# An encoder trunk: loads in another order, modulation chunks two slots later, bias masking in four pieces

## The reference

```
mod = silu(c) @ w_ada + b_ada                    # 1024 -> 6 x 1024, per sequence
sh1, sc1, gt1, sh2, sc2, gt2 = split(mod, 6)
hn = rmsnorm(x, g_mix) * (1 + sc1) + sh1
x  = x + gt1 * token_mixers(hn)
hn = rmsnorm(x, g_ffn) * (1 + sc2) + sh2
x  = x + gt2 * expert_choice_ffn(hn)
```

## Time and profile before

| | |
|---|---|
| time before, median of 3 runs | 2814.52 us (2800.98 to 2831.42) |
| profiled execution | 2833.76 us, span 2832.0 us, granted TensorE clock 0.899 |
| busy, share of the span | TensorE 87%, VectorE 66%, ScalarE 46%, POOL 13% |
| the chain that ended last, by engine | TensorE 76%, VectorE 9%, DMA 7%, issue 4% |
| DMA over the span | 599.38 MB, mean 212 GB/s |

### The profile page before, as it was taken

How to read it: one execution, slowest core, us unless ns; L and a number is a source line. 1 busy time by engine, 2 the same in 40 slices (tenths; PEclk the granted TensorE clock), 3 DMA queues, 4 the chain that set the end, 5 groups by cost and what they waited for, 6 DMA issues and landing times.

```text
span 2832.0 us, 31133 instructions
## 1 busy us (share of the span) xinstructions
PE 2469.0 (87%) x11606; PEld 1856.4 (66%) x11606; DVE 1856.3 (66%) x2984; ACT 1297.0 (46%) x2075; POOL 377.8 (13%) x253
## 2 busy tenths in 40 slices
PE   3978997969949999999969799698997699999993
PEld 1645775537737888888746467565775588888882
DVE  2535545535559999999844464454644899999994
ACT  1214323124307777777621243132431577777771
POOL 1011000101002111121100120001200011211112
PEclk8989888978969999999979797898987799999997
DMA  9055004060059999999860630322002899999994
GB/s 321 17 191 189 31 38 138 15 214 23 23 198 307 388 392 382 387 387 379 314 182 1 239 127 31 110 50 82 16 31 90 328 378 387 390 391 382 388 373 159
DMA packets 215461, 599.38 MB, mean 212 GB/s; under 512 B 36414, under 2 KB 51022, under 8 KB 215280
## 3 DMA queue, kind: packets, MB, share of 16 engines
q1 hardware_dynamic: 194496, 522.21, 49.6%
q0 software_dynamic: 15824, 58.27, 7.4%
q10 hardware_dynamic: 4992, 16.92, 1.6%
HBM read 555.62 MB, written 43.84 MB: 212 GB/s over the span
## 4 chain that ended last, share of the span: by engine, by line
PE 76%; DVE 9%; DMA 7%; issue 4%; ACT 1%; SPq 1%; POOL 1%; PEld 0%; POOLq 0%; DVEq 0%; PEldq 0%; ACTq 0%
PE bank L1407 12%; PE bank L1409 12%; PE bank L1408 12%; PE bank L1248 7%; PE bank L1317 5%; PE bank L1298 4%; DMA ring_a<-in_w_ada 3%; PE bank L1307 3%; PE bank L1341 3%; PE bank L1343 2%; PE bank L1342 2%; PE bank L1244 2%; PE bank L1246 2%; PE bank L1245 2%; DMA ring_w<-in_w_ada 2%
## 5 line engine op out<-in xcount | busy, mean ns | idle before, releaser
L1079 DVE TENSOR_TENSOR feed_lo<-feed,feed_hi 128x1024 fp32r<-128x1024 f32 x768 | 888.3, 1220 | 86.1 <-ACT feed_hi L718 84.4
L718 ACT ACTIVATE feed_hi<-feed 128x1024 fp32r<-128x1024 f32 x768 | 749.6, 1051 | 208.9 <-PE bank L1409 90.8
L1317 PE MATMUL bank<-V,pbuf 128*128 128x64 f32 x1664 | 251.5, 297 | 26.8 <-ACT pbuf L683 16.7
L1317 PEld LDWEIGHTS bank<-V,pbuf 128*128 128x128 f32 x1664 | 240.7, 219 | 39.0 <-ACT pbuf L683 25.3
L675 ACT ACTIVATE pbuf<-pbuf,smin 128x256 f32<-128x256 f32 (+2 forms) x192 | 117.3, 611 | 321.7 <-DVE smin L912 321.6
L1248 PE MATMUL bank<-ring,hT 128*128 128x512 f32 x512 | 228.3, 601 | 0.0
L476 POOL TENSOR_TENSOR stat<-stat,neg_half 128x1 f32<-128x1 f32 (+2 forms) x88 | 70.5, 801 | 1096.1 <-DVE stat L995 578.0
L1407 PE MATMUL bank<-feed_hi,hid_hi 128*128 128x512 f32 x512 | 204.9, 400 | 9.1 <-DVE hid_lo L1101 9.1
L1407 PE MATMUL bank<-feed_hi,merged_hi 128*128 128x512 f32 x512 | 207.2, 405 | 1.1 <-DVE merged_lo L1086 1.1
L1407 PE MATMUL bank<-feed_hi,xe_hi 128*128 128x512 f32 x512 | 204.9, 400 | 0.0
L1409 PE MATMUL bank<-feed_hi,merged_lo 128*128 128x512 f32 x512 | 204.1, 399 | 0.0
(11 more groups left out here) (190 smaller groups left out, 4117.4 us busy)
## 6 DMA issues: line engine op xcount, KB each, us to landing
feed<-in_w_gate SPq DMA_DIRECT2D x64, 2048.0 KB, 11.9
feed<-in_w_up SPq DMA_DIRECT2D x64, 2048.0 KB, 11.4
feed<-in_w_down SPq DMA_DIRECT2D x64, 2048.0 KB, 10.9
ring_a<-in_w_ada SPq DMA_DIRECT2D x40, 1024.0 KB, 5.2
...
X<-residual ACTq DMA_DIRECT2D x24, 512.0 KB, 3.5
...
```

What stands on the lines that cost most here:

```text
L718: act.activation(feed_hi[q % HIGHS][:, kk, :], feed[q % FEED][:, kk, :], ACT.Copy).then_inc(feed_hi_ready, 1)
L1079: dve.tensor_tensor(feed_lo[q % FEED][:, kk, :], feed[q % FEED][:, kk, :], full(feed_hi[q % HIGHS][:, kk, :]), ALU.subtract).then_inc(feed ...
L1317: ins = pe.matmul(bank[5 + oc // 512][:, oc % 512:oc % 512 + HD], pbuf[:, 3 + m % 2, b * P:(b + 1) * P], V[:, lo + b, vc:vc + HD], start=( ...
```

## The change

- First stage: the identity of `con` is loaded alone, the rest after POOL's memsets, with a semaphore of its own. X is loaded only after piece 1 has landed. The small rows are turned after the products with the pieces. `skew` is in two parts: `skew_pad` stays at the start, the writes of the DRAM table come after the first meeting.
- Masking: four instructions over 128 x 896 at slots 1, 3, 5 and 7, each of which waits until VectorE has done so many slots; VectorE waits for each at slots 12 to 15.
- Modulation chunks at slots 2n + 4 and 2n + 5, `mod_turn` at 20.
- SP after the projection: passes 1 to 3 all load the first chunk, w_out, the other chunks, then gate and rows; pass 4 as before.
- Layer seam: the chunks of w_in are loaded and, for tile 0, used in the order 1, 2, 3, 0.

In the diff, changes that only hand `it` on to `chunks` and `projected` are left out.

```diff
--- before.py
+++ after.py
@@ -102,6 +102,9 @@
 SLOTS = 16 * (TILES - 1) + AFTER[-1][0] + 1
 
 
+BIAS_AT = (1, 3, 5, 7)
+
+
 def streamed(layer, s):
 
     if s == 0:
@@ -119,15 +122,17 @@
     return 1 + layer * (SEQS + 2) + stage
 
 
-def chunks(i):
-
-
-    return (0, 1, 2, 3) if i == 0 else (2, 1, 0, 3)
-
-
-def projected(i, ch):
-
-    return MIX_CHUNKS * i + chunks(i).index(ch) + 1
+def chunks(it, i):
+
+
+    if i == 0:
+        return (1, 2, 3, 0) if it == SEQS else (0, 1, 2, 3)
+    return (2, 1, 0, 3)
+
+
+def projected(it, i, ch):
+
+    return MIX_CHUNKS * i + chunks(it, i).index(ch) + 1
 
 
 def schedule(layer, s):
@@ -136,9 +141,11 @@
     for k in range(SLOTS):
         out.append(("slot", k // 16, k))
         for n, c in enumerate(streamed(layer, s)):
-            out += [(name, c, k) for at, name in ((2 * n + 2, "ada_sum"), (2 * n + 3, "ada_turn")) if at == k]
-        if s == 0 and k == 19:
+            out += [(name, c, k) for at, name in ((2 * n + 4, "ada_sum"), (2 * n + 5, "ada_turn")) if at == k]
+        if s == 0 and k == 20:
             out.append(("mod_turn", 0, k))
+        if k in BIAS_AT:
+            out.append(("bias", BIAS_AT.index(k), k))
         for i in range(TILES):
             out += [(name, i, k) for at, name in AFTER if 16 * i + at == k]
     return out
@@ -254,7 +261,7 @@
         c_turned = sem("c_turned")
         pad_ready = sem("pad_ready")
         started = sem("started")
-        consts_in, passed = sem("consts_in"), sem("passed")
+        consts_in, rest_in, passed = sem("consts_in"), sem("rest_in"), sem("passed")
         arrived, released = sem("arrived"), sem("released")
         layer_in = sem("layer_in")
         skew_in, skew_out, bias_in = sem("skew_in"), sem("skew_out"), sem("bias_in")
@@ -374,7 +381,7 @@
 
                 for n, c in enumerate(streamed(layer, s)):
                     t = ada_turns(layer, s) + n
-                    if s == 0 and n == 1:
+                    if n == 1:
                         load_out(layer)
                     for h in range(2):
                         if n:
@@ -396,7 +403,7 @@
             for layer in range(LAYERS):
                 for s in range(SEQS):
                     it = layer * SEQS + s
-                    for n in range(MIX_CHUNKS):
+                    for n in (1, 2, 3, 0) if s == 0 and layer else range(MIX_CHUNKS):
                         if it == 0 and n >= 2:
                             sp.wait_ge(first_used, n + 1)
                         elif s == 0 and layer:
@@ -418,16 +425,13 @@
                                           [[127, GRID], [GRID * 128, 14], [1, GRID]])
                             sp.dma_start(bias_c[r * GRID:(r + 1) * GRID, h, :, :], src).then_inc(bias_in, 16)
                     sp.wait_ge(proj_used, it + 1)
-                    if s == 0:
-                        load_ada(layer, s)
-                    else:
+                    load_ada(layer, s)
+                    if not streamed(layer, s):
                         load_out(layer)
                     sp.wait_ge(mod_out, layer * 16 + 16)
                     sp.dma_start(gate[:, :], row_of(0, s, P)).then_inc(row_gate, 16)
                     sp.dma_start(rows2[:, 0, :], row_of(16, s, P)).then_inc(row_norm, 16)
                     sp.dma_start(rows2[:, 1, :], row_of(8, s, P)).then_inc(row_norm, 16)
-                    if s:
-                        load_ada(layer, s)
                 sp.wait_ge(row_used, layer * SEQS + SEQS)
                 for g in range(SEQS):
                     sp.dma_start(gate[64 * g:64 * g + 64, :], row_of(24, g, 64)).then_inc(row_gate, 16)
@@ -462,13 +466,14 @@
                 pool.sem_inc(released, 1)
 
             pool.dma_start(nat[0:2, 0:D], c[:, :]).then_inc(consts_in, 16)
-            pool.dma_start(con[:, :], consts[:, :]).then_inc(consts_in, 16)
+            pool.dma_start(con[:, 0:P], consts[:, 0:P]).then_inc(consts_in, 16)
             pool.memset(neg_half[:, :], -0.5).then_inc(started, 1)
             pool.wait_ge(started, 1)
             pool.memset(aff[:, :, :, :], 0.0).then_inc(started, 1)
             pool.wait_ge(started, 2)
             pool.memset(silu_c[:, :], 0.0).then_inc(started, 1)
             pool.wait_ge(started, 3)
+            pool.dma_start(con[:, P:C_END], consts[:, P:C_END]).then_inc(rest_in, 16)
 
             def powers(at, count, n):
 
@@ -476,15 +481,17 @@
                 pool.tensor_tensor(stat[:, 8 + at:8 + at + count], stat[:, at:at + count], neg_half[:, 0:count], ALU.pow)\
                     .then_inc(rstd_ready, 1)
 
+            def skew_pad(layer):
+
+                pool.memset(pads[layer][:, :], 0.0).then_inc(pad_ready, 1)
+                pool.wait_ge(pad_ready, layer + 1)
+                pool.dma_start(pads[layer][:, 48:48 + COL_OFF],
+                               rpb[layer:layer + 1, :, :, :].rearrange("l h r c -> (l h r) c")).then_inc(skew_in, 16)
+
             def skew(layer):
 
-                pad = pads[layer]
-                pool.memset(pad[:, :], 0.0).then_inc(pad_ready, 1)
-                pool.wait_ge(pad_ready, layer + 1)
-                pool.dma_start(pad[:, 48:48 + COL_OFF],
-                               rpb[layer:layer + 1, :, :, :].rearrange("l h r c -> (l h r) c")).then_inc(skew_in, 16)
                 pool.wait_ge(skew_in, layer * 16 + 16)
-                pool.dma_start(skew_d[:, :, :], pad[:, :].unsqueeze(1).to_broadcast([4 * ROW_OFF, GRID, 128])).then_inc(skew_out, 16)
+                pool.dma_start(skew_d[:, :, :], pads[layer][:, :].unsqueeze(1).to_broadcast([4 * ROW_OFF, GRID, 128])).then_inc(skew_out, 16)
 
             def prepare(layer):
 
@@ -507,18 +514,21 @@
                         n += 1
                         powers(0, 6, n)
 
-                pool.wait_ge(bias_in, it * 128 + 128)
-                bias = bias_c[:, :, :, :].rearrange("p h m c -> p (h m) c")
-                pool.tensor_tensor(bias, mask_c.unsqueeze(1).to_broadcast([P, 56, GRID]), bias, ALU.subtract)\
-                    .then_inc(bias_ready, 1)
                 if s and layer + 1 < LAYERS:
                     pool.wait_ge(proj_used, it + 1)
+                    skew_pad(layer + 1)
+                    pool.wait_ge(bias_in, it * 128 + 128)
                     skew(layer + 1)
                 if it == 0:
                     pool.dma_start(x_d[SEQ:SEQS * SEQ, :], x[SEQ:SEQS * SEQ, :]).then_inc(scattered, 16)
                 for kind, i, k in schedule(layer, s):
                     if kind == "slot" and KT <= k - SPLIT_FROM - 1 < 2 * KT:
                         split_out(pool, k - SPLIT_FROM - 1)
+                    if kind == "bias":
+                        pool.wait_ge(bias_in, it * 128 + 128)
+                        pool.wait_ge(biased, k)
+                        pool.tensor_tensor(bias_c[:, i, :, :], mask_c.unsqueeze(1).to_broadcast([P, 14, GRID]), bias_c[:, i, :, :],
+                                           ALU.subtract).then_inc(bias_ready, 1)
                     if kind == "heads_a":
                         n += 1
                         powers(0, 1, n)
@@ -555,9 +565,10 @@
                                             in_=xn[:, :] if e % 2 else nat[:, 0:D], in_offset=None,
                                             compute_op=ALU.add).then_inc(scattered, 16)
 
-            skew(0)
+            skew_pad(0)
             prepare(0)
             meet(epoch(0, 0))
+            skew(0)
             for layer in range(LAYERS):
                 for s in range(SEQS):
                     attend(layer, s)
@@ -593,6 +604,7 @@
                 for src, at, n in ((b_ada, R_BIAS, 48), (g_mix, R_GMIX, 8), (g_ffn, R_GFFN, 8), (g_grp, R_GGRP, 8)):
                     act.dma_start(rows[at:at + n, :], src[layer:layer + 1, :].rearrange("o (k p) -> (o k) p", p=P))\
                         .then_inc(rows_in, 16)
+            act.wait_ge(slot_loaded[ADA_SLOT[1]], 16)
             for i in range(TILES):
                 act.dma_start(X[i][:, :], x[i * P:(i + 1) * P, :]).then_inc(x_in[i], 16)
 
...
@@ -785,13 +797,13 @@
 
             def first_ada():
                 chain = Chain(dve, dve_done)
-                dve.wait_ge(vec_turned, 1)
-                chain.add(dve.tensor_copy(rows_t[:, :, :], bank[0][:, 0:LAYERS * R_END].rearrange("p (l r) -> p l r", r=R_END)))
                 for n in range(FIRST_ADA):
                     dve.wait_ge(first_used, n // 2 * 2 + 2)
                     if n >= 2:
                         dve.wait_ge(ada_turned, n - 1)
                     dve.tensor_copy(pbuf[:, n % 2, :], bank[2 + n % 4][:, :]).then_inc(ada_copied, 1)
+                dve.wait_ge(vec_turned, 1)
+                chain.add(dve.tensor_copy(rows_t[:, :, :], bank[0][:, 0:LAYERS * R_END].rearrange("p (l r) -> p l r", r=R_END)))
                 dve.wait_ge(ada_turned, FIRST_ADA)
                 chain.add(dve.tensor_tensor(mods[:, 0:M_GT1, :], bank[1][:, 0:M_GT1 * SEQS].rearrange("p (m s) -> p m s", s=SEQS),
```

(16 more changed lines are left out.)

10 lines of the change are left out of this document (5 added, 5 removed).

## The result

The kernel after takes 2793.34 us (median of 20 runs, 2772.56 to 2823.92) against 2829.59 us for the kernel before (median of 20 in the same comparison). The ratio is **0.9897** (95% interval 0.9874 to 0.992): faster by 1.0%, some 29 us. Forecast were 53.8 us off and 2761 us, with 2786 as the upper end; the direction was right, the size was not. The profiled execution of the changed kernel took 2787.26 us (span 2785.5, granted clock 0.908).

The account below looks back on a forecast made before the run. TensorE was taken to bound three quarters of the span, with waits elsewhere. Terms 13 + 19.8 (masking, three passes) + 6 + 1 + 13 + 2.5 - 1.5 = 53.8 us off gave 2761 us; range 2738 to 2786.

Parts of the forecast that it names:

- First stage: Kernel start: with the bias table's writes moved away, the fourth modulation piece lands near 32 us; 13 us off (5 to 15).
- the bytes-over-rate estimate of 30.3: First stage: 11.3 MB before the fourth modulation piece at 403 GB/s take 28 us, so it could land at 30.3 us.
- The mask: Each attention pass: masking in pieces lets TensorE's last transposes start earlier; 6.6 us a pass, less 1.5 for 16 pieces.
- Chunks two slots later, pass 1: First attention pass (layer 0, sequence 0): slots 0 to 20 take 70.15 us instead of 76.47; 6 us off (0 to 9).
- the long stall of the second chunk ... is what goes: Pass 1: the second modulation chunk's wait, queued behind w_out and a copy of x, disappears; part of the 6 us.
- Pass 3: Third attention pass (layer 1, sequence 0): later chunks give 1 us (-3 to 4), beside 6.6 us from the masking.
- Pass 2: Second attention pass (layer 0, sequence 1): second chunk at 594 us, slot 20 at 630.4; 13 us off (4 to 22), masking included.
- Layer seam: Between layers 0 and 1: new w_in chunk order gives faster scatter and reload, less a TensorE wait; 2.5 us off (-4.6 to 6.8).
- the 3.5 us for scatter and reload: Layer seam: last scatter and reload of X gain 3.65 and 3.2 us at most, 0 at least; middle taken, 3.5 us.
- The rule that was dismissed: Engines alternate between DMA queues packet by packet; by it the seam would give 4 us and the sum be 55.3.
- the pieces sit on VectorE's path: Rival, slots 1 to 8: all 16 masking pieces cost their 2 us; 24 us off, 2791 us, chance 0.08.
- The loads collide again: Rival: bias table's writes delay w_in's last chunk and pass 2's second chunk; 14 to 40 off, 2775 us, chance 0.17.

Follow-up runs that it names:

- chunks_early: Changed kernel with modulation chunks back at slots 2, 4, ... and the modulation's transpose at slot 19, new load order kept: 2796.22 us, 0.9903 of the kernel before.
- masks_only: Kernel before with only the masking changed, to four pieces in slots 1, 3, 5 and 7: 2809.41 us, 0.9946 of the kernel before.
- table_late: Changed kernel with layer 1's bias table written at slot 16 of pass 2 instead of at its head: 2804.89 us, 0.9884 of the kernel before.
- ahead: Changed kernel with w_out's first half and the first modulation chunk loaded inside the projection's last tile: 2800.31 us, 0.9874 of the kernel before.

## Why the prediction was right or wrong

**First stage: wrong, and the largest miss (13 forecast, 1.5 in the trace).** The step that failed is the sentence that POOL's 37.4% from 30 to 45 us "is mostly the bias table's writes". The row shows a queue, not what is in it. POOL's timeline and the DMA view from 11 to 30 us of the kernel before:

```profile
11.33 1.71 POOL L487 DMA_DIRECT2D bias_rows<-pad  x1 [6.94 <-DMA pad<-in_rpb]
```

```profile
bias_rows<-pad POOLq DMA_DIRECT2D x1, 1920.0 KB, 18.9
```

The table's write, issued at 11.33 us, landed 18.9 us later, and just then the queues slowed: they kept 403 GB/s as long as it ran, and the small loads stood behind it on POOL's queue. The change took the table away and left the small loads, which then held the queues from 12 to 25 us instead of 30 to 45. With them moved, the piece lands at 31.38, and the bytes-over-rate estimate of 30.3 was good.

**The mask: the mechanism right, its worth wrong.** TensorE's last transposes start 6.7 us earlier after the projection's end and slot 0 7.6 in every pass (6.6 forecast, 5 to 6.8), and the pieces cost nothing that shows: the add-and-minimum beside them takes 0.48 us. But the sum took this straight to the end. In passes 2 and 3 a chunk that stands behind w_out comes 30.4 and 22.9 us after the projection's end, with the mask's gain or without it. In pass 1 it did come 6.1 us earlier, with the copy of x that stood behind the masking out of its way. Alone the masking was worth 9.8 us at an equal clock instead of 26.

**Chunks two slots later, pass 1: wrong (6 forecast).** Mask and chunks together were to give 12.6 in pass 1; the trace has 6.3. The failed step is "the long stall of the second chunk ... is what goes". The chunk came 6.2 us earlier after the projection's end, with the copy of x out of its way, but TensorE reached it earlier too and waits, at whichever slot it stands: 6.23 us at slot 4 before, 6.15 at slot 6 after. So slots 0 to 20 took 73.75 instead of 70.15. The cycle was sized well (8.0 us from slot 8 to 20, forecast 8.21). The price of the modulation's transpose was put at 0.5 of a possible 3.7; slots 20 to 24 took 4.1 us longer. How much of that is the transpose is open: with it at slot 19, chunks_early comes to slot 24 only 1.8 us earlier (89.1 against 91.0).

**Pass 3: the sum right (7.6 forecast, 7.4), the split not.** The second chunk starts 22.88 us after the projection's end before and 22.87 after, so the mask's 6.6 did not arrive as such. Two more slots are done by then, but chunks_early, without them, comes to slot 24 as early (86.7 against 87.5). The clock from 40 to 60 us was 0.74 before and 1.00 in both of these; it moved slot 24 of this pass by 6.8 us between masks_only and chunks_early. How much of the 7.4 is the two slots and how much the clock, which would be luck, was not separated.

**Pass 2: right (13 forecast, 13.2 to slot 33).** Here the prediction did what the other passes lacked: it asked when the load could land and counted the mask within it. Its times count from the trace before, where the projection ends 7.8 us later (561.82 against 554.02). On that clock the second chunk's product started at 592.2 (594 forecast), slot 8 came at 598.2 (597.5) and slot 20 at 630.1 (630.4). The wait stands at slot 6, as forecast, and table_late shows that the table's write brought the chunk 7.5 us later; in ahead, with half of w_out loaded before, the wait was 8.10 instead of 16.48. What the higher clock gave (0.92 against 0.85 up to slot 33) is in the 13.2 too.

**Layer seam: wrong in sign (2.5 forecast, 0.6 lost).** The term that failed is the 3.5 us for scatter and reload: the reload gave back 0.9 of 3.2 us and the last scatter 0.1 of 3.65. The split was sized well: TensorE waited 0.85 us where I took 1. That the scatter beside chunks 1 to 3 takes 9.67 us was not foreseen, but it cost no time: the two scatters start 31.45 us apart before and after.

**The rule that was dismissed.** The trace says that from 14 to 20 us POOL's queue and SP's queue moved 89 packets each, POOL's 43 small ones counted, while their shares of the engines' time were 82.0% and 23.4%. The Trainium skill, "DMA: Bandwidth & Descriptors", section "Queues, rings and completion order", says that each engine takes the queues in turn, a packet at a time; the trace agrees with it. The prediction had read POOL's large share as speaking against that rule. It doesn't: with equal turns the queue with slow packets gets the most time and the other is held to its pace. At the seam the rule had given 4 us and a sum of 55.3, which the measured seam doesn't bear out either; what failed there were the scatter and the reload.

By the number the rival "the pieces sit on VectorE's path" (24 off, 2791, chance 0.08) came nearest, by luck: the pieces cost nothing that shows. "The loads collide again" (39 off, 2775) had the small first stage, for another cause than the one it named, and the table in front of pass 2's second chunk, but not pass 2's gain. One more thing moved the absolute number: 2814.52, the median of three runs, from which the sum was taken off, lies 15 us below the median of 20.
